# mLSTM scores of two heads at one place, and the turns of its output at other units, in a two-layer transformer pair

## The reference

```
mqk = silu(causal_depthwise_conv(concat([mq, mk])))          # 8 heads, 64 wide
hm  = mlstm_chunkwise(mq_c, mk_c, mv, mi + igate_b, mf + fgate_b)
ym  = sigmoid(mo) * rmsnorm(hm, mlstm_norm_w)
merged = g_a * (ya @ w_proj_a) + g_m * (ym @ w_proj_m)
x   = x + rmsnorm(merged @ w_out, mix_norm_post)
```

## Time and profile before

| | |
|---|---|
| median of 3 runs | 1938.76 us |
| profiled execution, its own time | 1938.86 us |
| its span, first to last instruction | 1936.8 us |
| PE busy | 1923.4 us, 99% |
| weight loads on PE | 1661.8 us, 86% |
| DVE busy | 1303.1 us, 67% |
| ACT busy | 1124.1 us, 58% |
| mean granted PE clock | 0.999 |

### The profile page before, as it was taken

One profiled execution on the slowest core, in us unless ns is written; L12 is line 12 of the kernel. 1 busy time (PEld: TensorE's weight loads), 2 busy tenths in 40 slices (PEclk: granted clock), 3 DMA queues, 4 the chain that ended last, 5 costly groups with the idle time before them and its releaser, 6 DMA issues.

```text
span 1936.8 us, 28378 instructions
## 1 busy us (share of the span) xinstructions
PE 1923.4 (99%) x10940; PEld 1661.8 (86%) x10940; DVE 1303.1 (67%) x2242; ACT 1124.1 (58%) x1797; POOL 6.5 (0%) x18
## 2 busy tenths in 40 slices
PE   9999999999999999999999999999999999999998
PEld 7888899899888888888989998888988888988887
DVE  5555787566655575558875666555858888858886
ACT  5444766554644564456774656445747666647665
POOL 0000000000000000000000000000000000000000
PEclk9999999999999999999999999999999999999999
DMA  8655545536555556655455456665535565535563
GB/s 280 187 186 184 172 132 168 169 126 201 193 186 188 180 181 189 186 162 174 138 168 165 152 164 215 186 192 153 167 114 188 184 187 180 168 115 187 184 188 96
DMA packets 93685, 335.75 MB, mean 173 GB/s; under 512 B 10224, under 2 KB 12528, under 8 KB 93552
## 3 DMA queue, kind: packets, MB, share of 16 engines
q1 hardware_dynamic: 92112, 328.51, 53.5%
q0 software_dynamic: 720, 4.37, 0.6%
q10 hardware_dynamic: 720, 1.07, 0.2%
HBM read 332.86 MB, written 1.05 MB: 172 GB/s over the span
## 4 chain that ended last, share of the span: by engine, by line
PE 92%; DVE 6%; ACT 1%; DMA 1%; issue 0%; SPq 0%; DVEq 0%; ACTq 0%
PE stream L1841 10%; PE stream L1843 9%; PE stream L1842 9%; PE acc L1841 9%; PE acc L1843 9%; PE acc L1842 9%; PE stream L2322 7%; PE stream L1835 7%; PE stream L1836 6%; PE stream L1837 6%; PE stream L2323 3%; DVE w_lo L1075 1%; PE stream L1935 1%; PE acc L2248 1%; PE acc L2045 1%; DVE conv_tiles L1540 1%
## 5 line engine op out<-in xcount | busy, mean ns | idle before, releaser
L1075 DVE TENSOR_TENSOR w_lo<-w_raw,w_hi 128x1024 fp32r<-128x1024 f32 x624 | 759.5, 1223 | 365.1 <-ACT w_hi L558 363.4
L558 ACT ACTIVATE w_hi<-w_raw 128x1024 fp32r<-128x1024 f32 x624 | 654.5, 1054 | 374.5 <-PE stream L1843 207.1
L1841 PE MATMUL stream<-w_hi,h_both 128*128 128x512 f32 x896 | 354.0, 395 | 0.0
L1843 PE MATMUL stream<-w_lo,h_both 128*128 128x512 f32 x896 | 349.2, 390 | 0.0
L1842 PE MATMUL stream<-w_hi,h_both 128*128 128x512 f32 x896 | 348.8, 389 | 0.0
L1835 PE MATMUL stream<-h_both,w_hi 128*128 128x256 f32 x800 | 234.4, 293 | 0.0
L1836 PE MATMUL stream<-h_both,w_hi 128*128 128x256 f32 x800 | 226.0, 282 | 0.0
L1837 PE MATMUL stream<-h_both,w_lo 128*128 128x256 f32 x800 | 225.9, 282 | 0.0
L2322 PE MATMUL stream<-h_both,w_hi 128*128 128x512 f32 x608 | 217.4, 400 | 0.0
L1841 PE MATMUL acc<-w_hi,act_hi 128*128 128x512 f32 x528 | 211.1, 400 | 1.6 <-DVE conv_sums L1532 1.3
L1843 PE MATMUL acc<-w_lo,act_hi 128*128 128x512 f32 x528 | 206.3, 391 | 0.0
(11 more groups left out here) (332 smaller groups left out, 2613.4 us busy)
## 6 DMA issues: line engine op xcount, KB each, us to landing
w_raw<-in_w_up SPq DMA_DIRECT2D x264, 512.0 KB, 3.5
w_raw<-in_w_mix SPq DMA_DIRECT2D x228, 512.0 KB, 3.5
w_raw<-in_w_down SPq DMA_DIRECT2D x132, 512.0 KB, 3.5
params<-in_params POOLq DMA_DIRECT2D x4, 859.5 KB, 6.7
out_x<-x_residual SPq DMA_DIRECT2D x4, 256.0 KB, 2.7
constants<-in_consts POOLq DMA_DIRECT2D x1, 832.0 KB, 7.4
x_residual<-in_x ACTq DMA_DIRECT2D x3, 256.0 KB, 6.7
x_residual<-in_x SPq DMA_DIRECT2D x1, 256.0 KB, 3.8
```

Source lines behind the costliest of these rows:

```text
L558: nc.scalar.activation(w_hi[:, u % RING], w_raw[:, u % RAW], ACT.Copy).then_inc(hi_ready, 1)
L1075: nc.vector.tensor_tensor(w_lo[:, u % RING], w_raw[:, u % RAW], w_hi[:, u % RING].bitcast(F32), ALU.subtract).then_inc(split_done, 1)
L1841: nc.tensor.matmul(dst, hi, w_hi[:, s, w], start=first, stop=False)
L1843: return nc.tensor.matmul(dst, hi, w_lo[:, s, w], start=False, stop=last)
```

## The change

- The scores of a pair of heads are made at one place: pairs at i = 48, 52, 56, 60 (`PAIR_AT`), and the values of heads 0 to 7 at i = 49, 50, 53, 54, 57, 58, 61, 62 (`NUM_AT`).
- The decay is in two banks: 256 columns in bank[3] (half of it for each head of the pair), selected over all 128 rows by a new tile `sel_low` that is zero on the upper half; 128 columns in the last quarter of side[h % 2], selected on the head's own row half. q.k goes to the first 384 columns of side[h % 2], the two heads by turns.
- `decay` has two buffers. The exponentials and `mlstm_p` of both heads come at the same step, and the exponentials also wait for `mlstm_qk`.
- The group's later steps are counted from `NUM_AT`: for the last group `take_num` at i = 62, `mlstm_stats` and `mlstm_rstd` at 63, `mlstm_out` at 64.
- `YM_TURN` becomes 63, 64, 66, 68. The first turn waits until bank[3] is read.
- Two small DVE instructions at the start of the first mixer fill `sel_low`; 64 bytes are left empty behind it.

```
-        zw, _ = sb("decay", [P, 3 * P])
+        zw, _ = sb("decay", [P, 2, 3 * P])
-        YM_TURN = (57, 63, 65, 68)
+        YM_TURN = (63, 64, 66, 68)
+        PAIR_AT = (48, 52, 56, 60)
+        NUM_AT = tuple(PAIR_AT[h // 2] + 1 + h % 2 for h in range(HEADS))
+        def early_decay(h):
+            return bank[3][:, h % 2 * T:h % 2 * T + T]
+        def late_decay(h):
+            return side[h % 2][:, 3 * P:]
+        def keys(h):
+            return side[h % 2][:, 0:3 * P]
...
-                    if i >= U_GL and i % 2 == 0 and i < U_GL + 16:
-                        mlstm_exp((i - U_GL) // 2)
+                    if i in PAIR_AT:
+                        mlstm_exp(2 * PAIR_AT.index(i))
+                        mlstm_exp(2 * PAIR_AT.index(i) + 1)
                     for g, (a, z) in enumerate(GROUPS):
-                        if i == U_GL + 1 + 2 * (z - 1):
+                        if i == NUM_AT[z - 1]:
                             take_num(g)
-                        if i == U_GL + 2 + 2 * (z - 1):
+                        if i == NUM_AT[z - 1] + 1:
                             mlstm_rstd(g)
...
+                    heads = (2 * p, 2 * p + 1)
+                    for h in heads:
+                        nc.tensor.matmul(early_decay(h), ident_r[:], neg_r[:, 0:T], start=True, stop=False)
+                        nc.tensor.matmul(late_decay(h), ident_r[:], neg_r[:, T:3 * P], start=True, stop=False)
+                        nc.tensor.matmul(early_decay(h), sel_low[:, h:h + 1].to_broadcast([P, P]), nm[:], start=False,
+                                         stop=True)
+                    for h in heads:
+                        r = slice(64 * (h % 2), 64 * (h % 2) + 64)
+                        nc.tensor.matmul(late_decay(h), sel_r[r, h:h + 1].to_broadcast([64, P]), nm[r, P:T], start=False,
+                                         stop=True).then_inc(mlstm_sc, 1)
+                    for c, ks, qs in ((slice(0, T), slice(0, P), slice(0, T)), (slice(T, 3 * P), slice(P, T), slice(P, T))):
+                        for h in heads:
+                            r = slice(64 * (h % 2), 64 * (h % 2) + 64)
+                            i = nc.tensor.matmul(keys(h)[:, c], y[r, 4 + h // 2, ks], y[r, h // 2, qs], start=True,
+                                                 stop=True)
+                            if c.start > 0:
+                                i.then_inc(mlstm_qk, 1)
...
                     if p == 0:
-                        pe.wait_ge(ya_split, l * 4 + 4)
+                        pe.wait_ge(mp_ready, n8 + HEADS)
```

More of the change, by code:

```diff
@@ L120, in build @@
         sel_r, _ = sb("row_select", [P, HEADS], F32R)
+        sel_low, _ = sb("low_select", [P, HEADS], F32R)
+        sb("low_select_pad", [P, 16])
         eps1, _ = sb("eps1", [P, 1])
@@ L726, in mlstm_exp @@
                     act.wait_ge(mlstm_sc, n8 + h + 1)
[L727 to L730, removed]
+                    act.wait_ge(mlstm_qk, n8 + h + 1)
+                    if h > 1:
+                        act.wait_ge(mp_ready, n8 + h - 1)
+                    nc.scalar.activation(zw[:, h % 2, 0:T], early_decay(h), ACT.Exp, bias=tok[:, h:h + 1])
+                    nc.scalar.activation(zw[:, h % 2, T:], late_decay(h), ACT.Exp,
                                          bias=tok[:, HEADS + h:HEADS + h + 1]).then_inc(mw_ready, 1)
@@ L1196, in prepare @@
                                                     ALU.mult)
+                        nc.vector.tensor_tensor(sel_low[0:64], ident[0:64, 0:HEADS], ident[0:64, 32:32 + HEADS], ALU.add)
+                        nc.vector.tensor_tensor(sel_low[64:P], ident[64:P, 0:HEADS], ident[64:P, 0:HEADS], ALU.subtract)
                         for b in (0, 64):
@@ L1338, in mlstm_p @@
                         dve.wait_ge(num_ready, n8 + h - 1)
-                    nc.vector.scalar_tensor_tensor(out=mp[:, h % 2], in0=side[0][:, 0:3 * P], scalar=A_SCALE,
-                                                   in1=zw[:], op0=ALU.mult, op1=ALU.mult).then_inc(mp_ready, 1)
+                    nc.vector.scalar_tensor_tensor(out=mp[:, h % 2], in0=keys(h), scalar=A_SCALE,
+                                                   in1=zw[:, h % 2], op0=ALU.mult, op1=ALU.mult).then_inc(mp_ready, 1)
                 def mlstm_stats(g):
@@ L1443, in mixer @@
                         conv(i - 1 - U_MQK)
-                    if U_GL <= i < U_GL + 16 and i % 2 == 0:
-                        mlstm_p((i - U_GL) // 2)
+                    if i in PAIR_AT:
+                        mlstm_p(2 * PAIR_AT.index(i))
+                        mlstm_p(2 * PAIR_AT.index(i) + 1)
                     for g, (a, z) in enumerate(GROUPS):
-                        if i == U_GL + 2 + 2 * (z - 1):
+                        if i == NUM_AT[z - 1] + 1:
                             mlstm_stats(g)
-                        if i == U_GL + 3 + 2 * (z - 1):
+                        if i == NUM_AT[z - 1] + 2:
                             mlstm_out(g)
@@ L2081, in ya_turn, with mlstm_scores @@
                     r.then_inc(ya_turned, 1)
-                def mlstm_scores(h):
-                    if h == 0:
+                def mlstm_scores(p):
+                    if p == 0:
                         pe.wait_ge(qk_silu, l + 1)
@@ L2087, in mlstm_scores @@
                         pe.wait_ge(sc_masked, (n8 + HEADS) * 2)
+                        pe.wait_ge(ya_split, l * 4 + 4)
                     else:
[L2089 to L2100, removed]
+                        pe.wait_ge(mp_ready, n8 + 2 * p)
@@ L2187, in mixer @@
                         g_tok()
[L2188 to L2191, removed]
+                    if i in NUM_AT:
+                        mlstm_values(NUM_AT.index(i))
+                    if i in PAIR_AT:
+                        mlstm_scores(PAIR_AT.index(i))
                     if i in YM_TURN:
```

## The result

The change made the kernel slower: 1951.65 us (median of 4 runs, 1951.25 to 1952.01) against 1938.97 us (4 runs of the kernel before on the same chip), a ratio of 1.0064 with a 95% interval of 1.0052 to 1.0076. The forecast was 1939.7 us, and the range ended at 1942.2. The profiled execution took 1951.25 us (before 1938.86), so there are 12.4 us to explain in the traces (12.7 by their spans, 1949.5 against 1936.8), and 12.7 by the medians.

What follows compares the result with a forecast made beforehand. The prediction took PE's own instructions as the bound in the mLSTM stage. From 1938.86 us, -5.1 for the pairs and +6.0 for the waits gave 1939.8, or 1939.7 us by the median, range 1933.4 to 1942.2.

Steps and rivals of the forecast that it cites:

- The layout: Tiles behind sel_low shift by 128 bytes: given nothing, a few tenths of a us either way as bounds.
- The clock: Rival: PE's two stalls drop the clock to 1.2 GHz, 2.88 us more each, 1945.5 us in all; chance 0.07.
- The wait: PE stands still before unit 64 until turn 0's split is ready: 3.0 us per layer, 6.0 us in all.
- The pairs: mLSTM scores of two heads together: 1.80 us per pair against 2.44, eight pairs saving 5.1 us (3.8 to 6.2).
- Values, `mlstm_p`, `take_num`, later turns: mLSTM stage on PE: values and turns keep their price, these inputs arrive in time, no second wait; no cost.
- No wait: Rival: turn 0's split is there when turn 1 wants it, 1933.7 us; chance 0.13, half lengths included.
- The halves don't overlap: Rival: keys of a pair's two heads run one behind the other, 5.2 us in all, 1944.9 us; chance 0.06.

Runs made afterwards that it cites:

- e4: The kernel before with 128 empty bytes behind row_select and nothing else changed: 1946.43 us, ratio 1.0036.
- e2: The changed kernel with YM_TURN = (62, 64, 66, 68), turn 0 one unit earlier, layout as changed: 1942.0 us, ratio 1.0013.
- e3: The changed kernel with low_select behind all other tiles, no padding, and YM_TURN = (62, 64, 66, 68): 1934.58 us, ratio 0.9975.
- e1: The changed kernel with low_select behind all other tiles and no padding, so older tiles keep their addresses: 1942.48 us, ratio 1.0018.
- e5: The kernel before with 256 empty bytes behind row_select: 1939.59 us, ratio 1.0001.
- e7: The kernel before with 128 empty bytes ahead of all tiles, so that all move together: 1939.58 us, ratio 1.0001.
- e10: The kernel before with YM_TURN = (57, 64, 65, 68) instead of (57, 63, 65, 68): 1948.07 us, ratio 1.0046.
- e8: The changed kernel, low_select behind all tiles, with ACT's ym_round(0) ahead of mlstm_rstd(2) in step 63: 1938.47 us, ratio 0.9996.
- run 528: Not a follow-up run: "run" is a verb here, and 528 is the number of matmuls in a group of the down projections; no time belongs to it.
- e9: The kernel before with 128 empty bytes ahead of all tiles and 128 more behind w_lo: 1956.46 us, ratio 1.0088.
- e6: The kernel before with 64 empty bytes behind row_select: 1943.43 us, ratio 1.0021.
- e11: The changed kernel with YM_TURN = (62, 64, 66, 68) and without the 64 bytes behind low_select: 1938.06 us, ratio 0.9995.
- e12: The changed kernel with YM_TURN = (62, 64, 66, 68) and 192 bytes behind low_select: 1934.98 us, ratio 0.9978.

## Why the prediction was wrong, point by point

- **The layout, given nothing: this step failed.** "No tile changes its place modulo 128 and no access its shape, so I give it nothing (a few tenths either way as bounds)". The bounds had no row behind them. The term measured 7.1 us in the trace, 6.9 alone (e4), 7.4 within the changed kernel (e2 against e3). It falls on matmuls in parts of the kernel that the change doesn't touch.
- **The clock, kept at its upper level: this step failed.** It stood among the rivals at 0.07, with 5.8 us as its price. It measured 4.5 us in the profiled execution and 3.8 to 4.3 by the medians. I judged by one row, 2.79 us of idle near the end of the run with the clock at 1.00 in the window behind it. The row says that of its one us in its one execution, and it was no bound. The same stretch, 2.79 or 2.80 us, stands near the end of every profile, and in four of the other thirteen (e1, e5, e7, e10) the granted clock was at its lower level when PE got going again. PE's timeline and the window behind the wait, from e5:

```profile
1930.91 1.97 PE L2244 MATMUL stream<-constants,y_tok 128*128 128x128 f32 x8 [2.80 <-ACT y_tok L851]
```

```profile
1930.91:1931.91 1.00, 1.00 (x5) 1.00 (x6) 0.00 (x0) 0.00 (x0) 0.00 (x0) 0.50 0.00 0
```

The eight matmuls took 1.97 us there and 1.09 in the row that I went by. e1 shows the like within one execution: one wait of 2.92 us without a fall, and one with it. The Trainium skill's rule (page "TensorE: Matmul & The Clock Gate", section "Why this matters for your kernels"), that idle gaps between bursts of matmuls let the clock fall to half, came true here, and I had set it aside for that one row.
- **The wait, priced at 3.0 us per layer: right.** 2.93 and 2.92, in front of unit 64, released by `ym_lo`, nowhere else. e8 took one link out and left 1.50. ACT's wait for the statistics is 2.75 us again, and `ym_hi` stands right behind `mlstm_rs`; then DVE:

```profile
419.85 0.30 ACT L763 ACTIVATE mlstm_rs<-mlstm_var,eps 128x4 f32<-128x4 f32 x1 [2.75 <-DVE mlstm_var L1379]
420.18 0.21 ACT L766 ACTIVATE mlstm_rs<-mlstm_rs 128x4 f32<-128x4 f32 x1
420.29 0.82 ACT L772 ACTIVATE ym_hi<-stream,params 128x256 fp32r<-128x256 f32 x2
```

```profile
421.15 0.88 DVE L1402 SCALAR_TENSOR_TENSOR ym_lo<-stream,params,ym_hi 128x256 fp32r<-128x256 f32 x2 [1.33 <-ACT ym_hi L772]
```

- **The pairs, priced at a saving of 5.1 us: right, a little high.** 4.7 from the timeline, 4.9 by e3. By its parts: masks and selections over all rows with the going over to 64 rows 360.63 - 359.84 = 0.79 (0.70 + 0.09 forecast), which is partly luck; the row-half selections 0.17 (0.06, within its ends of 0.03 and 0.18); the keys 0.79 (0.85); the return 0.10 (0.10). Within the 0.79 two errors cancel. The late mask of 128 columns is followed by the next matmul after 0.06, the lower end, where I had taken 0.11; and a selection with `sel_low` is followed by the next mask after 0.17 (360.19 - 360.02), where I had taken 0.12. My upper end for a pair was also added up wrongly: its terms give 1.94 and not 1.97, which moves the lower end of the saving from 3.8 to 4.0 us and changes nothing else.
- **Values, `mlstm_p`, `take_num`, later turns at no cost: right.** The list of waits has none of them, and turn 2 follows without one.
- **The rivals.** "No wait" didn't come, but e3 shows what it is worth once the layout is taken out as well: 1934.6 measured, 1933.7 by that rival's sum. "The halves don't overlap" is refuted by 0.79 us for two heads' keys.

With the two failed terms at their measured sizes the sum would have been 1938.8 - 4.7 + 5.9 + 4.5 + 7.1 = 1951.6, against 1951.65.

## What to carry to other kernels

A new tile at the head of a memory plan moves every tile behind it, and where matmuls run 528 at a time a few ns each are more than the edit itself: allocate it behind everything else, or compare the costliest groups of untouched lines before and after. A term that is held at zero needs a row as much as any other. And price an idle stretch of PE at its length plus the clock behind it: one such stretch that went unpunished in one execution says little, as the same stretch in other executions shows.

## What the runs showed of the hardware that I had not expected

- A matmul of 512 columns takes a few ns more or less by where its stationary tile, and what lies with it, is in SBUF against the streamed weights. With `act_lo` stationary the median start distance is 227 ns as before and after shifts of 256 bytes or of both sides together, 231 or 232 ns if one of them moves by 128 against the other (e9, e4), and 234 ns by 64 (e6). It behaves like a relation modulo 256 bytes, by shifts of 64, 128 and 256; other shifts weren't tried. The internal reason stays open. Since 64 bytes sped up the second block's group without moving either of its tiles (e6), accesses of other engines to tiles that did move may have a part in it; that wasn't tried.
- Behind a wait of 2.92 or 2.93 us the clock fell in 5 of the 6 cases of the profiled executions (after, e1, e10), for 3.41 or 6.83 us, and each of the two lengths came in either layer. It came between 1.0 us ahead of PE's restart (after, layer 1) and 1.3 us behind it (e1, layer 1). It didn't fall behind 1.50 us (e8, both layers). Behind the 2.79 or 2.80 us near the end of the run the clock was down at PE's restart in 4 of the 14 profiles and fell before the eight matmuls behind it had ended in three more (after, e11, e12). What decides between 3.41, 6.83 and none was not found.
